# Gathering an expert's rows in transposed form: normed x becomes the stationary operand and the one-hot matrix moves

## What is computed

```python
h = rms_norm(x, norm2_g[l]) * (1.0 + sc2) + sh2
x = x + g2 * moe_ffn(h, router_w[l], router_b[l], w_gu[l], b_gu[l], w_down[l], b_down[l])

def expert_block(args):
    xe, eid = args
    gu = xe @ w_gu[eid] + b_gu[eid]
    g, u = jnp.split(gu, 2, axis=-1)
    g = jnp.minimum(g, SWIGLU_LIMIT)
    u = jnp.clip(u, -SWIGLU_LIMIT, SWIGLU_LIMIT)
    act = (u + 1.0) * (g * jax.nn.sigmoid(SWIGLU_ALPHA * g))
    return act @ w_down[eid] + b_down[eid]
```

## Time and profile before

| | us |
|---|---|
| median of 3 runs (1343.43, 1343.65, 1348.52) | 1343.65 |
| the profiled execution's own time | 1342.69 |
| its span from first to last instruction | 1340.7 |
| TensorE busy | 1277.4 (95%) |
| TensorE weight loads busy | 591.0 (44%) |
| VectorE busy | 518.2 (39%) |
| ScalarE busy | 187.1 (14%) |
| share of TensorE in the chain that ended last | 71% |
| share of the weight transfers (down, gate-up) in that chain | 17%, 6% |

### The profile page before, as it was taken

One profiled execution on the slowest core, in us unless ns is written; L12 is line 12 of the kernel. 1 busy time (PEld: TensorE's weight loads), 2 busy tenths in 40 slices (PEclk: granted clock), 3 DMA queues, 4 the chain that ended last, 5 costly groups with the idle time before them and its releaser, 6 DMA issues.

```text
span 1340.7 us, 16852 instructions
## 1 busy us (share of the span) xinstructions
PE 1277.4 (95%) x5991; PEld 591.0 (44%) x5992; DVE 518.2 (39%) x1160; ACT 187.1 (14%) x377; POOL 15.7 (1%) x48
## 2 busy tenths in 40 slices
PE   5999999999999999999998999999999998899997
PEld 3866866778753333333333333333333333233332
DVE  3032665332234443344334333434344344334344
ACT  2101322332021001100011000001000011001002
POOL 0000000110000000000000000000000000000000
PEclk9999999999999999999999999999999999999999
DMA  9858675316678999999999999999999999799994
GB/s 353 318 188 295 221 244 182 126 64 245 231 287 319 425 427 428 429 429 429 427 428 429 429 429 426 376 429 429 430 427 429 427 430 428 316 430 426 429 429 205
DMA packets 59183, 477.55 MB, mean 356 GB/s; under 512 B 4991, under 2 KB 5076, under 8 KB 32532
## 3 DMA queue, kind: packets, MB, share of 16 engines
q1 hardware_dynamic: 58852, 476.11, 86.4%
q10 hardware_dynamic: 304, 1.06, 0.2%
HBM read 476.10 MB, written 1.05 MB: 356 GB/s over the span
## 4 chain that ended last, share of the span: by engine, by line
PE 71%; DMA 23%; DVE 3%; issue 2%; SPq 1%; ACT 0%; DVEq 0%; ACTq 0%
PE bank L1601 21%; DMA down_ring<-in_w_down 17%; PE bank L1638 14%; PE bank L1283 11%; DMA gu_ring<-in_w_gu 6%; PE bank L1429 4%; PE bank L1276 4%; PE bank L1567 3%; PE bank L1589 3%; PE bank L1331 2%; PE bank L1492 2%; PE bank L1559 1%; PE bank L1390 1%; DVE scratch L1114 1%; DVE scratch L1112 1%
## 5 line engine op out<-in xcount | busy, mean ns | idle before, releaser
L1601 PE MATMUL bank<-gu_ring,scratch 128*64 128x512 f32 x2048 | 461.9, 597 | 7.0 <-DMA gu_ring<-in_w_gu 5.3
L1601 PEld LDWEIGHTS bank<-gu_ring,scratch 128*64 128x64 f32 x2048 | 143.3, 137 | 292.6 <-issue 282.7
L1638 PE MATMUL bank<-down_ring,scratch 128*64 128x512 f32 x1024 | 233.8, 598 | 22.3 <-DMA down_ring<-in_w_down 17.2
L1283 PE MATMUL bank<-gu_ring 128*128 128x256 f32 x640 | 143.8, 381 | 0.0
L1638 PEld LDWEIGHTS bank<-down_ring,scratch 128*64 128x64 f32 x1024 | 70.5, 136 | 143.5 <-issue 130.7
L1283 PEld LDWEIGHTS bank<-gu_ring 128*128 128x128 f32 x640 | 119.8, 190 | 18.6 <-issue 1.3
L701 ACT ACTIVATE scratch<-bank 128x512 f32<-128x512 f32 x32 | 19.1, 597 | 690.0 <-PE bank L1601 690.0
L1102 DVE TENSOR_TENSOR scratch<-bank,bgu 128x512 f32<-128x512 f32 x32 | 22.1, 691 | 225.7 <-PE bank L1567 225.7
L1070 DVE TENSOR_TENSOR xres<-xres,bank 128x512 f32<-128x512 f32 x132 | 81.8, 681 | 60.1 <-PE bank L1589 60.1
L1567 PEld LDWEIGHTS bank<-ident,scratch 128*128 128x128 f32 x392 | 41.1, 140 | 79.5 <-ACT scratch L705 26.0
L1559 PE MATMUL bank<-xn,onehot 128*64 128x512 f32 x264 | 69.6, 605 | 0.0
(11 more groups left out here) (265 smaller groups left out, 819.9 us busy)
## 6 DMA issues: line engine op xcount, KB each, us to landing
gu_ring<-in_w_gu SPq DMA_DIRECT2D x128, 2048.0 KB, 25.3
down_ring<-in_w_down SPq DMA_DIRECT2D x64, 2048.0 KB, 18.9
gu_ring<-in_w_in SPq DMA_DIRECT2D x32, 1024.0 KB, 7.8
gu_ring<-in_w_ada SPq DMA_DIRECT2D x16, 1024.0 KB, 7.1
down_ring<-in_w_ada SPq DMA_DIRECT2D x8, 512.0 KB, 10.2
gu_ring<-in_w_ada SPq DMA_DIRECT2D x8, 512.0 KB, 11.5
gu_ring<-in_w_pa SPq DMA_DIRECT2D x4, 1024.0 KB, 6.2
gu_ring<-in_w_pb SPq DMA_DIRECT2D x4, 1024.0 KB, 6.5
```

The costliest lines, as they stand in the source:

```text
L1283: last = M(dst[:, b * T:(b + 1) * T], group_chunk(group, kt // 4)[:, kt % 4, cols], hT[:, kt, :], start=kt == 0, stop=kt == KT - 1)
L1601: last = M(bank[f // 2][64 * a:64 * a + 64, :], xT[:, kt % 4, kt // 4, :], gu_ring[:, 8 * half + kt, f * 512:(f + 1) * 512], start=kt == 0 ...
L1638: last = M(bank[7][64 * a:64 * a + 64, :], act_sb[:, kt % 4, kt // 4, :], down_ring[:, kt // 2, (kt % 2) * D + a * 512:(kt % 2) * D + (a + ...
```

## The change

The gather is written the other way round. For each block of 128 columns of x (the columns have stride 2), the stationary operand is normed x (128 tokens x 128 columns) and the one-hot matrix (64 columns) moves, so that the product is the gathered rows already transposed, 128x64, in bank 6. A block takes two matmuls (two token tiles) and there are 8 blocks: `take(item, 0)` does four of them ahead of the transposes of u, `take(item, 1)` the other four behind. ScalarE's copy of the gathered rows and the four transposes in the middle of the down product are gone from the loop. The first item, gathered ahead of the loop, keeps the old form (`take_first`, `copy_first`). In a further pass the transposed rows go to bank 3 in place of bank 6, which is now in use for the next item, so two waits move or are added there, and the wait for ScalarE's copy falls away. SyncE's last load of `final_g` over `xn` waits for the new semaphore.

```diff
-            sp.wait_ge(taken_done, NE + 1)
+            sp.wait_ge(takenT_done, NE + 1)
...
                 A(in_blocks(u_raw), by_fours(bank[1][:, :]), ACT.Copy).then_inc(raw_ready, 1)
-                copy_taken(item + 1)
                 copy_back(item)
...
-                taken = bank[6][:, 0:KT * FCAP].rearrange("p (c q s) -> p c q s", c=2, q=4)
+                taken = bank[3][:, 0:KT * FCAP].rearrange("p (c q s) -> p c q s", c=2, q=4)
...
-            def take(item, tiles=range(TT), early=False):
+            def take(item, a):
+
+                pe.wait_ge(onehot_ready, item + 1)
+                for j in range(4):
+                    first, at_ = a * 512 + j // 2 * 2 * P + j % 2, (2 * j + a) * CAP
+                    for tt in range(TT):
+                        last = M(bank[6][:, at_:at_ + CAP], xn[:, tt, first:first + 2 * P - 1:2], onehot[:, tt, :],
+                                 start=tt == 0, stop=tt == TT - 1, skip_group_check=True)
+                if a:
+                    last.then_inc(takenT_done, 1)
+
+            def take_first(tiles, early=False):
...
-            def take_transposed(item):
-                pe.wait_ge(xraw_ready, item + 1)
-                transposes(6, x_raw).then_inc(takenT_done, 1)
...
                 pe.wait_ge(given_added, item * 4 + 4)
-                take(item + 1, (0,))
+                take(item + 1, 0)
                 pe.wait_ge(raw_ready, item * 2 + 2)
                 transposes(3, u_raw).then_inc(uT_done, 1)
-                take(item + 1, (1,))
+                take(item + 1, 1)
                 way_back(item)
                 further_passes(pe, item, count, lambda b, k: further(item, half, fills, k))
                 for kt in range(KT):
-                    if kt == KT // 2:
-                        take_transposed(item + 1)
...
             def further(expert, half, fills, k):
 
-                pe.wait_ge(xraw_ready, expert + 2)
                 pe.wait_ge(f_onehot, (expert + k) * 2 + 2)
...
                 pe.wait_ge(f_xraw, k + 1)
+                pe.wait_ge(act_ready, expert * 2 + 2)
+                pe.wait_ge(f_mark, k + 1)
                 for c in range(2):
-                    last = nc.tensor.transpose(bank[6][:, c * P:(c + 1) * P], f_x[:, c * P:(c + 1) * P], ident[:])
+                    last = nc.tensor.transpose(bank[3][:, c * P:(c + 1) * P], f_x[:, c * P:(c + 1) * P], ident[:])
                 last.then_inc(f_takenT, 1)
-                pe.wait_ge(f_mark, k + 1)
                 pe.wait_ge(f_xT_ready, k + 1)
```

More of the change, by code:

```diff
@@ L692, in in_blocks, with copy_first @@
                 return columns.rearrange("s (j p) -> s j p", p=P)
-            def copy_taken(item):
-                act.wait_ge(taken_done, item + 1)
+            def copy_first():
+                act.wait_ge(taken_done, 1)
                 A(x_raw.rearrange("s (b r p) -> s b r p", b=2, r=2), by_pairs(bank[4][:, :]), ACT.Copy).then_inc(xraw_ready, 1)
@@ L719, in further @@
                 A(sig[:, :, :, 0:FCAP], g_sb[:, :, :, 0:FCAP], ACT.Sigmoid, scale=ALPHA).then_inc(f_sig, 1)
-            copy_taken(0)
+            copy_first()
             copy_back(-1)
@@ L1555, in take @@
                 else:
-                    pe.wait_ge(onehot_ready, item + 1)
+                    pe.wait_ge(onehot_ready, 1)
                 for tt in tiles:
@@ L1691, in further @@
                       ).then_inc(f_given, 1)
-            take(0, (0,), early=True)
+            take_first((0,), early=True)
             keep_busy(3, 6)
@@ L1700, in _ @@
             keep_busy(2, 6)
-            take(0, (1,))
+            take_first((1,))
             pe.wait_ge(over_ready, 1)
@@ L1706, in _ @@
             way_back(-1)
-            take_transposed(0)
+            pe.wait_ge(xraw_ready, 1)
+            transposes(6, x_raw).then_inc(takenT_done, 1)
             pe.wait_ge(passes_ready, 1)
```

## The result

| | before | after |
|---|---|---|
| median of 6 runs each, us | 1346.25 (1343.43 to 1348.52) | 1354.43 (1353.17 to 1358.32) |
| profiled execution: own time, span, us | 1342.69, 1340.7 | 1355.85, 1353.8 |
| TensorE busy, weight loads busy | 1277.4 (95%), 591.0 (44%) | 1311.5 (97%), 685.3 (51%) |
| ScalarE busy | 187.1 (14%) | 171.3 (13%) |
| share of TensorE in the chain that ended last | 71% | 94% |

The ratio is 1.0071, with the interval [1.0055, 1.0088]: 0.7% slower. That is 8.2 us between the medians, where 5.1 were forecast, and past the 0.5% that part "slower" from "the same".

The account below looks back on a forecast made before the run. Transfers bound items 7 to 15 and, after a restart, up to 1127.22 us; TensorE bounds the start and everything behind. Terms +1.2, 0, 0, +0.4 and +3.5 sum to +5.1 us: median 1348.8 us, range 1343.5 to 1358.0.

Parts of the forecast that it names:

- Added: In the gather: sixteen matmuls, 32 records, paced by weight loads at 0.111 us a record, 3.56 us in all.
- Rival 1: In the gather: stationary weights read with stride 2 load slower, some 0.03 us a record; 1357.9 us, chance 0.13.
- The stretch as a whole: From the gather's start to the down product's: 4.51 us after, 3.18 before; the item ends 0.58 us later.
- Start, +1.2: Item 1's down transfer is released 1.33 us later, leaving the transfers idle for about 1.2 us.
- Items 1 to 15, 0: TensorE needs 27.95 us an item, under the transfers' 29.37; item 15's 1.37 us wait just covers the delay: 0.
- Items 16 to 25, "transfers again": Up to 1127.22 us in item 25 transfers set the pace, so the change adds 0.
- Item 25, +0.4: Gather stretch 4.51 us against 2.94, less 0.43 for ScalarE's copy, less 0.75 for the transposes: +0.4 us.
- Items 26 to 31, +3.5: Six whole items at the end, bound by TensorE, each 0.58 us longer: +3.5 us.
- No overlap of load and stream (2): In the gather: loads and streams run one after the other, 1.7 us more an item; 1395 us, chance 0.05.
- The clock in the gather (3): The gather uses the array lightly, so the clock falls; items 2.5 us longer, 1401 us, chance 0.05.
- Quicker loads (4): In the gather: loads at 0.093 us a record, 0.6 us less an item; about 1345 us, chance 0.15.
- the stream alone (5): In the gather: moving columns alone set the pace, 0.75 us an item gained; 1338 us, chance 0.05.

Follow-up runs that it names:

- s1: The changed kernel run again with no edit: 1354.91 us, ratio 1.0075 to the kernel before.
- s2: The changed kernel with its code shifted by 32 tiny matmuls at the opening of TensorE's program: 1350.72 us, ratio 1.0047 to the kernel before.
- s3: The kernel before, without the four transposes inside the down product in the loop, so experts work on other rows: 1342.68 us, ratio 0.9989.
- s4: The changed kernel with contiguous columns of x (stride 1, not 2) as stationary operand, which are not the columns needed: 1350.02 us, one run.
- s6: The changed kernel with only 32 of the 64 one-hot columns moving in each gather product: 1372.77 us, one run.
- s5: The kernel before with its code shifted by 22 tiny matmuls at the start of TensorE's program: 1352.94 us, ratio 1.0056.
- s7: The kernel before with the order of transfers on the SyncE queue changed over at item 6 in place of 16: 1349.62 us, ratio 1.0034.
- s8: The changed kernel with the order of transfers changed over at item 6 in place of 16: 1365.65 us, ratio 1.0146 to the kernel before.

## Why the prediction was right and wrong

**The median** (1348.8 forecast, 1354.43 measured) lies within the range given (1343.5 to 1358.0), but the likeliest case, "the same" with 0.66, did not come; "slower", with 0.31, did. Some 3 us of the excess is the stop in item 1, by the stretches of s1 and s2. Without the stop s2 lies 5.0 us over the kernel before by the medians and 6.3 (0.47% of 1345) by its ratio, whose interval reaches from 3.9 to 8.6; the forecast had 5.1. That the measured median is within the range is luck in part: the range reached to 1358.0 for slower loads, and what used it up is a stop that no term and no rival names.

**Removed: right in size.** 0.75 us an item, and s3 measured 0.73. What the forecast did not say is that a saving alone would hardly have reached the end: s3 shows that the transfers take over before it.

**Added: the mechanism right, the size a little short.** The step that failed is "0.111 a record": it measured 0.118. Rows 5's L1509 has no stride; s4 without stride gives exactly 0.111, and s6 shows that the moving columns don't matter below 64. Rival 1 was the true one in kind, with 0.03 us a record in place of 0.007. It took all of 0.55 - 0.42 us for the stride; but the loads of L1577, which have none, take 0.48 us where they stand behind the gather's loads (1220.37) and 0.42 alone, so nearly half of that difference needs no stride. The stretch as a whole came to 4.53 us for 4.51, and that near hit is luck: s4, whose loads do come at the forecast's 0.111, takes 4.33, so the terms for the changes of shape were 0.2 us too large and hid the stride's 0.2. Then there is 0.11 us more ahead of the stretch: the last gate-up products and the change of shape before the gather take 1.87 us (1216.68 to 1218.55) for 1.76 before (1207.12 to 1208.88). So an item costs 0.72 us net, not 0.58; without the stride it would be 27.89 - 27.37 = 0.52.

**VectorE's wait is covered: right.** No wait named VectorE stands before the down product any more in a whole item.

**Start, +1.2: wrong, the term is near 0.** (By its own figures it should have been 1.3: the down data began behind the gate-up data's end already.) In s2, which has no stop, the down transfer of item 1 was issued 21.23 us after the first gate-up issue; before, it was 432.23 - 412.45 = 19.78. So the delay, of 1.45 us, is there. But item 15's down data landed 446.7 us after that first issue in s2 (834.78 + 25.38 - 413.48) and 447.1 before (834.10 + 25.40 - 412.45). The step that failed is "take 4.9 us each (2.1 MB at 428 GB/s), so they end near ... 433.35". Stretches of the kernel before, then of s2, as the earlier trace rows:

```profile
412.45:426.00 13.55, 13.55 (x64) 4.56 (x64) 4.86 (x11) 1.60 (x3) 0.00 (x0) 1.00 0.93 349
...
434.00:436.00 2.00, 2.00 (x12) 0.72 (x10) 0.23 (x1) 0.00 (x0) 0.00 (x0) 1.00 1.00 369
```

```profile
413.48:427.00 13.52, 13.52 (x64) 4.79 (x65) 4.84 (x11) 1.57 (x3) 0.00 (x0) 1.00 0.93 345
...
435.00:437.00 2.00, 2.00 (x12) 0.65 (x10) 0.00 (x0) 0.00 (x0) 0.00 (x0) 1.00 0.99 340
```

The rate over the first 13.55 us is 349 GB/s and not 428, so the four transfers end more than a microsecond later than I worked out, near 434.7, and the down data (from 433.5 on) had that much cover. With the change the cover is used up and the dip between them goes from 369 to 340 GB/s for 2 us: 0.3 and 0.4 us of transfer time, not 1.2 more. This is read from the stretches; no run tried it by itself.

**Items 1 to 15, 0: right,** save for the stop in item 1, which could not be read from any row of the kernel before. Of the transfers that stood in the chain item after item one is left; it lands at 865.90 us, and item 15's two halves then wait nothing and 1.04 us for it, where the earlier trace rows have 1.37 and 0.72:

```profile
840.50 25.40 DMA down_ring<-in_w_down
```

```profile
861.34 3.65 PE L1642 MATMUL bank<-down_ring,scratch 128*64 128x512 f32 x16
...
866.03 3.65 PE L1642 MATMUL bank<-down_ring,scratch 128*64 128x512 f32 x16 [1.04 <-DMA down_ring<-in_w_down]
```

The thin cover of which the forecast spoke was used: of 5.4 us of stop and slow clock, and whatever the start added, 2.4 are left at item 16.

**Items 16 to 25, "transfers again": nearly right, for a reason that has passed.** The gate-up wait of 1.77 us in item 25 is gone:

```profile
1127.80 8.80 PE L1607 MATMUL bank<-gu_ring,scratch 128*64 128x512 f32 x40
...
1143.52 1.07 PE L1653 MATMUL bank<-xn,f_pick 128*32 128x256 f32 x16
...
1145.27 0.44 PE L1667 MATMUL bank<-ident,scratch 128*128 128x128 f32 x2 [0.31 <-ACT scratch L712]
...
1157.82 5.34 PE L1685 MATMUL bank<-down_ring,scratch 128*32 128x512 f32 x32 [2.62 <-DVE scratch L1153]
```

TensorE had some 4.3 us of slack over these items and the 1.77 of that wait, 6.1 in all, and nine items and a part use 9 x 0.72 = 6.5 and a little more. The transfers' reserve is just used up: TensorE now bounds from item 16 to the end. The cost so far was under 1 us, but from here on each further tenth in an item would count sixteen times and not six.

**Item 25, +0.4.** From item 16's piece to item 26's it is 2.46 us longer in all. Of that 1.7 is the down product of the further pass, 5.34 us for 3.64 before, at a fallen clock. That isn't the change: s5 and s7, with the old gather, have 4.96 and 5.34 there, and s4, with the new one, has 3.64. What is left, 0.8 us, stands to +0.4 and the 0 of the items before. The wait of 0.43 us for ScalarE is gone, as forecast, but TensorE now waits 0.31 us for ScalarE two steps later (1145.27, L1667).

**Items 26 to 31, +3.5:** 6 x 0.72 = 4.3, measured 4.2 in the change and 4.3 in s2.

**The rivals.** No overlap of load and stream (2) would have given 0.165 us a record and items of 29.7 us: out, at 0.118 and 28.09. The rule behind it, of the Trainium skill, "TensorE: Matmul & The Clock Gate", under "The mechanism", is thus not what these rows show: all row groups are in use, and the loads hide the whole stream of 64 columns. (The same section of the Trainium skill also lets a load run ahead when it goes to "the background weight buffer"; that would fit the rows, and no run here tells whether it is the reason.) The clock in the gather (3): out for 64 columns, true for 32. Quicker loads (4) and the stream alone (5): out by the pace. What the list lacked is a rival that has nothing to do with the engines' work: the program's code itself.

## What to carry to other kernels

Work that leaves one form for another on the same engine is worth its difference only where that engine ends last: here 0.75 us an item came off and 1.47 came on, and even the first alone would have bought at most some 0.3%, since transfers take over before the end. Before a kernel with a loop is called slower or faster by half a per cent, look at the first pass through the loop for stops named "issue", and run it once more with its code shifted by a few harmless instructions; that shift was worth 0.3% in one kernel here (the two intervals overlap a little) and 0.6% in the other. And don't judge a stretch safe for the clock by the engine's busy time: in s6 it was busy all through the stretch behind which the clock fell.

## What the runs showed of the hardware that I had not expected

- TensorE stood 3.2 to 4.4 us, with nothing to wait for, in the first pass through the loop (items 0 and 1 are one body of it), in the change and in s1, s4, s5, s6 and s8, of which s5 has the old gather; in the kernel before and in s2, s3 and s7 not at all. Packets of 16 KB on an instruction queue come beside the stops, while the weights fill the queues at 426 GB/s; none comes in later items of the change. The Trainium skill, "Runtime: NRT & Kernel Launch", under "Instruction fetch mechanics", says that instructions are fetched in 16 KiB blocks, and the cost of passing from one to the next is "mostly hidden". The packets' size agrees; the cost, here, is hidden or 3 to 4 us by where the code lies. In all seven stops TensorE goes on 2.4 to 2.7 us after the packet's start (in the change 463.64 and 466.27 us), while the stops are 3.2 to 4.4 us long: their ends keep closer to the packet than to their own beginnings. That the packet's late arrival makes the stop is still a reading of time and place, shown by moving code and not by moving packets. Six of the seven stops stand just behind the place where TensorE's program jumps over the code of the further pass (`further_passes`), between `way_back` and the down product, and the seventh three records after it. Whether that jump is why the packet comes late no run tried; how the fetch is scheduled stays open.
- A stop of 4 us lengthens its item by more than itself: the clock was 0.61 over the next 4 us, and the transfers, whose slots came free late, ran at 98 GB/s over 4 us behind it.
- Weight loads of 128 rows and 128 columns start 0.111 us apart without stride and 0.118 with a stride of 2, alike for 32 and 64 moving columns.
- With 32 moving columns a record, 4.3 us of gather let the clock fall in about every other item (0.57 over the next 4 us); with 64 the clock of the same place was 1.00.
